# The feed-forward plan: six gate tiles first, and an up unit directly behind each down product

## The reference, cut to what matters

```python
h = rmsnorm(x, ln2[l])
gate = causal_dwconv(h @ w_gate[l], ffn_conv[l])      # 1024 -> 2816, then 3 taps along the tokens
x = x + (jax.nn.silu(gate) * (h @ w_up[l])) @ w_down[l]
return rmsnorm(x, ln_f)
```

## Time and profile before

| | us |
|---|---|
| median of three runs (lowest, highest) | 2668.59 (2666.81, 2672.78) |
| the profiled execution: time, span | 2666.36, 2664.5 |
| busy in the span: TensorE, VectorE, ScalarE, GpSimd | 2474.7, 1385.3, 1022.0, 504.5 |

### The profile page before, as it was taken

The page is one execution under the profiler, slowest core; times in us unless marked ns, Lnnn a source line. Parts: engine busy times, 40 slices in busy tenths (PEclk is TensorE's granted clock), DMA queues, the critical chain, the costliest instruction groups (busy, mean ns, idle before and its releaser), DMA issues.

```text
span 2664.5 us, 36444 instructions
## 1 busy us (share of the span) xinstructions
PE 2474.7 (93%) x14220; PEld 1524.5 (57%) x14220; DVE 1385.3 (52%) x2603; ACT 1022.0 (38%) x1944; POOL 504.5 (19%) x342
## 2 busy tenths in 40 slices
PE   6998887899999999797969999999899998999998
PEld 4874566433333333675744434443677887788887
DVE  3596545335444445586442333333766654673745
ACT  5225552234444443626523222222453343442423
POOL 0222102001111011233100000000324311453533
PEclk9999999899999999899989999999999998999999
DMA  7215714689999998420039999999122011132221
GB/s 279 68 48 222 285 64 180 245 326 380 386 388 385 388 387 347 145 79 17 33 134 394 421 421 421 421 421 403 55 92 80 17 32 48 56 111 92 99 95 64
DMA packets 85514, 567.98 MB, mean 213 GB/s; under 512 B 11640, under 2 KB 12024, under 8 KB 20320
## 3 DMA queue, kind: packets, MB, share of 16 engines
q1 hardware_dynamic: 79944, 550.27, 52.4%
q0 software_dynamic: 3616, 11.80, 2.0%
q10 hardware_dynamic: 1784, 3.58, 0.4%
HBM read 550.92 MB, written 14.68 MB: 212 GB/s over the span
## 4 chain that ended last, share of the span: by engine, by line
PE 44%; DVE 3%; DMA 2%; ACT 1%; POOL 1%; issue 1%; DVEq 0%; ACTq 0%; POOLq 0%
PE PS L1193 11%; PE PS L1322 3%; PE PS L1323 3%; PE PS L1324 3%; PE PS L1310 2%; PE PS L1308 2%; PE PS L1309 2%; PE PS L1267 2%; PE PS L1298 2%; PE PS L932 1%; PE PS L1555 1%; PE PS L1557 1%; PE PS L1556 1%; DMA RF<-in_w_down_dram 1%; PE PS L1440 1%
## 5 line engine op out<-in xcount | busy, mean ns | idle before, releaser
L3004 POOL TENSOR_TENSOR WHL<-RING,WHL 128x1024 fp32r<-128x1024 f32 (+1 forms) x84 | 203.4, 2422 | 822.4 <-ACT WHL L1590 818.3
L1590 ACT ACTIVATE WHL<-RING 128x1024 fp32r<-128x1024 f32 (+1 forms) x158 | 149.8, 961 | 238.2 <-PE PS L1324 134.1
L1193 PE MATMUL PS<-RING,RF 128*64 128x512 f32 x816 | 187.2, 602 | 1.0 <-issue 0.7
L1193 PE MATMUL PS<-WIDE,RF 128*64 128x512 f32 x792 | 182.0, 596 | 0.0
L2169 DVE TENSOR_TENSOR WHL<-RING,WHL 128x1024 fp32r<-128x1024 f32 (+1 forms) x74 | 97.8, 1323 | 129.1 <-ACT WHL L1590 124.7
L1883 ACT ACTIVATE RF<-PS,MODS,MSC 128x128 f32<-128x128 f32 x192 | 73.2, 445 | 180.1 <-PE PS L1267 128.8
L1308 PE MATMUL PS<-RR,WHL 128*128 128x512 f32 x336 | 136.6, 406 | 3.7 <-DVE RR L2700 1.8
L1310 PE MATMUL PS<-RR,WHL 128*128 128x512 f32 x336 | 133.6, 398 | 0.0
L1309 PE MATMUL PS<-RR,WHL 128*128 128x512 f32 x336 | 132.6, 395 | 0.0
L1193 PE MATMUL PS<-RF 128*64 128x512 f32 x544 | 127.5, 596 | 0.4 <-DMA RF<-in_w_down_dram 0.4
L1193 PE MATMUL PS<-X,RF 128*64 128x512 f32 x528 | 123.0, 597 | 0.4 <-DMA X<-in_w_down_dram 0.4
(11 more groups left out here) (446 smaller groups left out, 5752.1 us busy)
## 6 DMA issues: line engine op xcount, KB each, us to landing
RING<-in_w_gate_dram SPq DMA_DIRECT2D x63, 1024.0 KB, 8.8
WIDE<-in_w_down_dram SPq DMA_DIRECT2D x52, 1024.0 KB, 11.9
RING<-in_w_up_dram SPq DMA_DIRECT2D x46, 1024.0 KB, 8.6
RING<-in_ada_w_dram SPq DMA_DIRECT2D x44, 1024.0 KB, 6.5
AR<-in_w_up_dram SPq DMA_DIRECT2D x37, 1024.0 KB, 10.4
X<-in_w_gate_dram SPq DMA_DIRECT2D x36, 1024.0 KB, 8.8
RF<-in_w_down_dram SPq DMA_DIRECT2D x31, 1024.0 KB, 13.8
RING<-in_w_in_dram SPq DMA_DIRECT2D x30, 1024.0 KB, 5.0
```

The source lines that it names most:

```text
L1193: ins = e.matmul(a[r:r + 64, :], xs[:, j, 0:64], w[:, i, :], start=begin and i < 2, stop=end and i > 1)
L1590: e.activation(h, unsplit(st), ACT.Copy).then_inc(act, A(("hi", st["i"])))
L3004: e.tensor_tensor(lo, unsplit(st), h.bitcast(F32), ALU.subtract).then_inc(pool, G(("lo", st["i"])))
```

## The change

The order becomes: six gate tiles, unit 0, then two gate tiles ahead of each next unit, but none ahead of unit 4 and unit 8, which follow a down product directly; gates 20 and 21 come ahead of unit 10. The sums for units 4 and 8 stand behind the low parts of the down product's second half. In a gate step the convolution of an earlier gate, if one is left, comes ahead of the sums in the plan. The fourth operand moves from unit 0 to gate 4. In `low` a part is now put one step later only where the step at which it is made is a product; at gate and down steps it is made in the same step as its high part. A convolution of gate f > 5 waits for `gl` of the unit that used its buffer before.

```diff
 def ffn_order():
-    ends = {t1 // 2 - 1: part for part, (t0, t1) in enumerate(FFN)}
-    order = [("gate", 0), ("gate", 1)]
-    for u in range(FFN[-1][1] // 2):
-        if u + 1 < FFN[-1][1] // 2:
-            order += [("gate", 2 * u + 2), ("gate", 2 * u + 3)]
-        order += [("product", u, p) for p in SEVEN]
-        if u in ends:
-            order += [("down", ends[u], 0), ("down", ends[u], 1)]
+    order, gates = [], 0
+    for part, (t0, t1) in enumerate(FFN):
+        for u in range(t0 // 2, t1 // 2):
+            while gates < min(u + 3 - part, FFN[-1][1] // 2) and not (part and u == t0 // 2):
+                order += [("gate", 2 * gates), ("gate", 2 * gates + 1)]
+                gates += 1
+            order += [("product", u, p) for p in SEVEN]
+        order += [("down", part, 0), ("down", part, 1)]
     return order

 def ffn_plan():
-    plan = []
-    for what, *k in ffn_order():
+    plan, order, folded = [], ffn_order(), 0
+    for n, (what, *k) in enumerate(order):
+        following = next((it[1] for it in order[n:] if it[0] == "product"), None)
         if what == "down":
             plan += [(what, *k)]
+            if k[1] and following is not None:
+                plan += [("sum", following, i) for i in (1, 2, 3, 4)]
             continue
         plan += [("w",), (what, *k)]
         if what == "gate":
             f, = k
-            if f > 1:
-                u = f // 2 - 1
-                plan += [("sum", u, 1 + f % 2 * 2), ("sum", u, 2 + f % 2 * 2)]
-            if f % 2 or f == 2:
-                plan += [("conv", f - 1), ("silu", f - 1)]
-            if 0 < f < 4:
-                plan += [("operand", {1: 5, 2: 6, 3: 7}[f])]
+            if folded < f:
+                plan += [("conv", folded), ("silu", folded)]
+                folded += 1
+            if following > f // 2 - 3 and order[n + 2 - f % 2][0] == "product":
+                plan += [("sum", following, 1 + f % 2 * 2), ("sum", following, 2 + f % 2 * 2)]
+            if 0 < f < 5:
+                plan += [("operand", {1: 5, 2: 6, 3: 7, 4: 4}[f])]
         else:
             u, p = k
-            last = FFN[-1][1] // 2 - 1
-            plan += {1: [("conv", 2 * u + 3), ("E", u), ("silu", 2 * u + 3)] if u < last else [("E", u)],
-                     2: [("operand", 4)] if u == 0 else [],
...
-            if u == last - 1 and p in (6, 5):
-                plan += [("sum", last, i) for i in ((1, 2) if p == 6 else (3, 4))]
+            if p == 1 and order[n - 1][0] == "gate":
+                plan += [("conv", folded), ("E", u), ("silu", folded)]
+                folded += 1
+            elif p == 1:
+                plan += [("E", u)]
...
@@ in weight_steps
-            late = n >= len(ahead) - (len(steps) - ffn) and loads[st["load"]]["name"] != "w_down2"
+            used = n - (len(ahead) - len(steps))
+            late = used >= ffn and steps[used]["single"]
             low[n + late].append(st)
@@ VectorE, "conv"
                     e.wait_ge(pe, P["gate", f])
+                    if f > 5:
+                        e.wait_ge(dve, V["gl", f // 2 - 3])
```

More of the change, by code:

```diff
@@ L126, in ffn_plan @@
             f, = k
-            if f > 1:
-                u = f // 2 - 1
-                plan += [("sum", u, 1 + f % 2 * 2), ("sum", u, 2 + f % 2 * 2)]
-            if f % 2 or f == 2:
-                plan += [("conv", f - 1), ("silu", f - 1)]
-            if 0 < f < 4:
-                plan += [("operand", {1: 5, 2: 6, 3: 7}[f])]
+            if folded < f:
[5 more added lines that the diff above has]
+                plan += [("operand", {1: 5, 2: 6, 3: 7, 4: 4}[f])]
         else:
             u, p = k
-            last = FFN[-1][1] // 2 - 1
-            plan += {1: [("conv", 2 * u + 3), ("E", u), ("silu", 2 * u + 3)] if u < last else [("E", u)],
-                     2: [("operand", 4)] if u == 0 else [],
-                     6: [("U2", u), ("C11", u)], 7: [("UB", u), ("C22", u)], 4: [("UC", u), ("gu", u), ("gh", u), ("gl", u)]}.get(p, [])
-            if u == last - 1 and p in (6, 5):
-                plan += [("sum", last, i) for i in ((1, 2) if p == 6 else (3, 4))]
+            if p == 1 and order[n - 1][0] == "gate":
[3 more added lines that the diff above has]
+                plan += [("E", u)]
+            plan += {6: [("U2", u), ("C11", u)], 7: [("UB", u), ("C22", u)],
+                     4: [("UC", u), ("gu", u), ("gh", u), ("gl", u)]}.get(p, [])
     return plan
```

## The result

The changed kernel takes 2681.16 us (median of 6 runs, 2678.35 to 2684.76) against 2668.53 beside it: ratio 1.0044, 95% interval 1.0032 to 1.0056, so slower by 0.3 to 0.6%, 8.5 to 14.9 us.

The account below looks back on a forecast made before the run. Feed-forward part bound by TensorE's matmuls, which the change leaves equal. Start -2.4, end -2.0, rounds +15.2 and down products +6.0 make +16.8 on 2666.36: 2683.2, plus 0.8 for timed runs, 2684 us; range 2668 to 2694.

Parts of the forecast that it names:

- The rounds: Eight ordinary rounds: TensorE waits 1.9 us in each for product 7's low part, +15.2 us.
- The down products: First two down products: TensorE waits 2.35 us for the second weight step, plus slow clock, +6.0 us.
- The end: End of the feed-forward part: the last unit's 1.9 us wait goes, -2.0 us.
- The start: Start of the feed-forward part: six gates ahead save 4.9 us, less 2.5 for unit 0's late product 7, -2.4 us.
- Rival 1: At sum 2 and behind it: VectorE goes first or seldom meets GpSimd; 2662 us, faster, chance 0.08.
- Rival 4: At the start: six gates give nothing since VectorE is no earlier for unit 0; 2686 us, no chance of its own.
- Rival 3: At 11 stalls: the clock falls at every new one, +13 us, 2697 us; chance 0.12.

Follow-up runs that it names:

- sums_first: The changed kernel, but GpSimd makes sums 1 and 2 of a unit ahead of the first gate step's low parts; 2671.82 us, ratio 1.0014.
- conv_first: The changed kernel, but from gate 7 VectorE runs the previous gate's convolution ahead of the second gate step's low parts; 2670.32 us, ratio 1.0012.
- down_low_early: The changed kernel, but the down product's low parts are made in the step of their high part; 2677.16 us, ratio 1.0034.
- sums_first_down_early: The changed kernel with both repairs: sums 1 and 2 ahead of the low parts, down steps' low parts with their high part; 2661.90 us, ratio 0.9979.
- new_low_rule_only: The kernel before, with its order and plan, given only the changed rule of `low`; 2693.19 us, ratio 1.0094.

## Why the prediction was right

The way was as put on record, and so were place and mechanism at the rounds, the down products and the end, though not at the start; the predicted 2684 is 3 us above the measured 2681.16. Term by term, from the two profiled executions:

- *The rounds*, +15.2 predicted: eight waits, from start to start 1.47 to 1.72 us longer than the usual step, 13.4 together, and 0.8 for the slower first step behind each: 14.2. The chain went as worked out to 0.2 us: sum 2 at S+10.1 (predicted 10.1), the low parts of 6 and 5 done at S+13.6 (13.65), TensorE at S+18.7 (18.8).
- *The down products*, +6.0: waits of 2.24 and 2.22 (2.35 predicted), 4.8 from start to start, and slow clock behind the first alone, 1.6 us: 6.4.
- *The end*, -2.0: the wait of 1.9 has gone.
- *The start*, -2.4: this term was mis-sized, and that its wait came out as assumed was luck. From gate 3's start to the next gate or unit behind gate 5 and unit 0 it took 31.35 us (2305.91 to 2337.26) against 31.8, so -0.5. The wait of unit 0 was the 2.5 I had assumed, but the slow clock of 1.5 us behind it was only in the bound and not in the value. In sums_first, conv_first, down_low_early and sums_first_down_early, where the same wait was followed by no slow clock, the same part of the order took 29.7 to 29.9, about -2. And the wait was made in another way than I had worked out. Product 7's low part is done 25.4 us behind gate 3's start, where TensorE wants it at 22.8. With the old rule, the same work and the same six gates it is done at 23.2 and leaves no wait, since TensorE comes there only at 23.3, having lost 0.6 by the wait ahead of gate 4 and the slower restart behind it. The 2.2 between 25.4 and 23.2 are two VectorE instructions, an operand and a small low part, first in the changed kernel, then with the old rule:

```profile
2317.06 1.79 DVE L2174 TENSOR_TENSOR WHL<-RING,WHL 128x512 fp32r<-128x512 f32 x1
...
2322.73 2.31 DVE L2960 TENSOR_TENSOR AS<-AR,AS 128x1024 fp32r<-128x1024 f32 x1 [1.65 <-ACT AS L2141]
```

```profile
2320.10 1.23 DVE L2959 TENSOR_TENSOR AS<-AR,AS 128x1024 fp32r<-128x1024 f32 x1 [1.65 <-ACT AS L2140]
2321.24 0.69 DVE L2173 TENSOR_TENSOR WHL<-RING,WHL 128x512 fp32r<-128x512 f32 x1
```

In the changed kernel GpSimd ran a low part at 2317.01 and a sum at 2322.66 beside them; with the old rule it stood idle at both. So collisions made 2.2 us of the delay and VectorE's own work some 0.5, where I had put 1.1 on that work and the rest on collisions at the four small parts.

The sum of these is 18.1, the stretch grew by 18.2, and 16.8 was predicted. That the median grew by 12.6 only is not settled. The stretch began 2.1 us earlier in the profiled execution of the changed kernel, and the 1.5 us of slow clock in unit 0 may be that execution's alone. So that 2684 lies as near as 3 us to the median is in part luck. Rival 1 (the port decides the other way) fell: VectorE went second at both d.2. Rival 4 is the one the start came near to, for another reason than I gave. Rival 3 (the clock falls at every new stall) was half right at the three long waits, where it fell behind two, and wrong at the nine short ones.

## What to carry to other kernels

Where several engines run fixed programs in order, a rule that moves a small step earlier on one of them must be read for what stands behind it: product 2's low part was not needed sooner, and it held two sums and through them a convolution on another engine. Before an order is judged, hold the rule fixed and change the order, then the other way round; here the order was worth 0.3% of the kernel and the rule, which came in the same change, cost more than that. And an engine that is busy a little over half the time (VectorE, 52% of the span) can still be what ends last in a stretch, when its queue is in the wrong sequence.

## What the runs showed of the hardware

The same wait is followed by a slow clock in one place and not in another. Behind the wait of 2.24 us at the first down product the granted clock of the changed kernel was 0.55 in the mean of 3 us, behind that of 2.22 at the second it was 1.00 (stages behind either: the granted clock is the third figure from the end). In new_low_rule_only, with 2.24 at both, it stayed up at the first and fell at the second.

```profile
2414.40:2417.40 3.00, 3.00 (x8) 2.38 (x9) 0.94 (x1) 0.00 (x0) 0.00 (x0) 0.55 0.68 191
2543.00:2546.00 3.00, 3.00 (x14) 2.43 (x13) 0.69 (x1) 0.00 (x0) 0.00 (x0) 1.00 0.74 243
```

Over the profiles of this case there are 15 waits of 2.2 to 2.6 us in the stretch; behind 9 of them, the clock fell to its lower level (1.2 GHz) for a time, at 1.2 to 1.6 us lost each, behind 6 it did not, and behind none of the waits of 1.3 to 1.9 us did it. The Trainium skill (TensorE: Matmul & The Clock Gate, Part 1) says of the clock's rise that its moment varies from run to run, since the chip's own watch runs free of the kernel. These rows show that a fall in the middle of a kernel varies too; what decides it is not shown here.

The other is how evenly VectorE and GpSimd hold each other up. In the profiles of the kernel before, the changed one, sums_first and conv_first in the ordinary rounds, a small low part of VectorE of 0.69 us took 1.78 or 1.79 behind `gl`, whether the GpSimd instruction beside it was a sum (before) or a low part (the others).
